# Expert tails as plain fp32 products in four column groups, and 160 rows per visit

## The reference

```
logits = h @ router_w + router_b                 # 1024 tokens, 32 experts
top_vals, top_idx = top_k(logits, 4); gates = softmax(top_vals)
for each expert e, on the tokens that chose it:
    gu  = x @ w_up[e] + b_up[e]                  # 1024 -> 2048
    glu = min(gu[:, :1024], 7); lin = clip(gu[:, 1024:], -7, 7)
    hid = glu * sigmoid(1.702 * glu) * (lin + 1)
    y   = hid @ w_down[e] + b_down[e]            # 1024 -> 1024
out[token] += gate * y
```

## Time and profile before

| what | value |
|---|---|
| time, median of 3 runs (lowest to highest) | 2607.01 us (2598.25 to 2608.39) |
| time of the profiled execution | 2605.41 us |
| its span, first to last instruction | 2603.6 us |
| mean granted TensorE clock | 0.954 |
| PE busy | 2385.3 us, 92% |
| DVE busy | 1812.7 us, 70% |
| ACT busy | 1293.2 us, 50% |
| HBM read and written | 484.37 MB and 41.68 MB |

### The profile page before, as it was taken

One profiled execution on the slowest core, in us unless ns is written; L12 is line 12 of the kernel. 1 busy time (PEld: TensorE's weight loads), 2 busy tenths in 40 slices (PEclk: granted clock), 3 DMA queues, 4 the chain that ended last, 5 costly groups with the idle time before them and its releaser, 6 DMA issues.

```text
span 2603.6 us, 38978 instructions
## 1 busy us (share of the span) xinstructions
PE 2385.3 (92%) x13604; PEld 1938.2 (74%) x13605; DVE 1812.7 (70%) x1928; ACT 1293.2 (50%) x1445; POOL 363.5 (14%) x305
## 2 busy tenths in 40 slices
PE   6999986699989977999999999999999999999993
PEld 4889864598748955777777777777777777777772
DVE  4699778514142465978877777778777778988763
ACT  5412364313231344766655555566555556766553
POOL 0000000010003011212112211221122112222111
PEclk8999987599999978999999999999999999999996
DMA  4111310310101148989978787689787789998775
GB/s 140 65 49 50 113 51 18 130 57 33 49 1 29 66 150 290 356 293 331 351 256 292 249 296 256 230 279 324 258 285 251 244 282 310 351 362 306 249 240 161
DMA packets 263968, 527.23 MB, mean 202 GB/s; under 512 B 10908, under 2 KB 45008, under 8 KB 263536
## 3 DMA queue, kind: packets, MB, share of 16 engines
q1 hardware_dynamic: 246976, 470.49, 51.3%
q0 software_dynamic: 15008, 52.70, 8.7%
q10 hardware_dynamic: 1904, 2.90, 0.4%
HBM read 484.37 MB, written 41.68 MB: 202 GB/s over the span
## 4 chain that ended last, share of the span: by engine, by line
PE 80%; DVE 8%; issue 6%; ACT 4%; DMA 1%; DVEq 1%; ACTq 0%; POOLq 0%; POOL 0%; SPq 0%
PE PS L2528 12%; PE PS L2530 12%; PE PS L2529 12%; PE PS L2094 9%; PE PS L2536 7%; PE PS L2533 6%; PE PS L2326 4%; PE PS L2424 4%; PE PS L2133 2%; DVE wlo L1886 2%; PE PS L2498 1%; PE PS L2386 1%; PE PS L2552 1%; PE PS L2351 1%; PE PS L2353 1%
## 5 line engine op out<-in xcount | busy, mean ns | idle before, releaser
L1886 DVE TENSOR_TENSOR wlo<-raw,whi 128x2048 fp32r<-128x2048 f32 x387 | 880.0, 2288 | 202.6 <-ACT whi L1128 182.1
L1128 ACT CAST whi<-raw 128x2048 fp32r<-128x2048 f32 x387 | 730.0, 1911 | 174.2 <-PE PS L2536 137.1
L2528 PE MATMUL PS<-whi,xhi 128*128 128x512 f32 x1024 | 426.4, 416 | 1.2 <-DVE wlo L1886 1.2
L2529 PE MATMUL PS<-wlo,xhi 128*128 128x512 f32 x1024 | 399.9, 391 | 1.8 <-issue 1.8
L2530 PE MATMUL PS<-whi,xlo 128*128 128x512 f32 x1024 | 401.4, 392 | 0.0
L2530 PEld LDWEIGHTS PS<-whi,xlo 128*128 128x128 f32 x1024 | 192.9, 188 | 44.4 <-issue 2.0
L2528 PEld LDWEIGHTS PS<-whi,xhi 128*128 128x128 f32 x1024 | 194.2, 190 | 40.8 <-DVE wlo L1886 7.5
L2529 PEld LDWEIGHTS PS<-wlo,xhi 128*128 128x128 f32 x1024 | 193.4, 189 | 38.7
L2528 PE MATMUL PS<-whi,hhi 128*128 128x512 f32 x512 | 203.5, 397 | 8.8 <-DVE wlo L1886 8.8
L2530 PE MATMUL PS<-whi,hlo 128*128 128x512 f32 x512 | 200.4, 391 | 0.0
L2529 PE MATMUL PS<-wlo,hhi 128*128 128x512 f32 x512 | 200.1, 391 | 0.0
(11 more groups left out here) (400 smaller groups left out, 4563.3 us busy)
## 6 DMA issues: line engine op xcount, KB each, us to landing
raw<-in_exp_w_up SPq DMA_DIRECT2D x259, 1024.0 KB, 5.1
raw<-in_exp_w_down SPq DMA_DIRECT2D x128, 1024.0 KB, 6.9
ring<-in_w_in SPq DMA_DIRECT2D x11, 1024.0 KB, 5.5
xres<-in_x SPq DMA_DIRECT2D x4, 1024.0 KB, 10.3
ring<-in_xattn_wk SPq DMA_DIRECT2D x4, 1024.0 KB, 9.1
ring<-in_xattn_wv SPq DMA_DIRECT2D x4, 1024.0 KB, 6.2
ring<-in_w_out SPq DMA_DIRECT2D x4, 1024.0 KB, 7.2
xres<-in_x SPq DMA_DIRECT2D x1, 4096.0 KB, 20.9
```

Source lines behind the costliest of these rows:

```text
L1128: nc.scalar.copy(whi[:, chunk_slot(c, NSPL), :], raw[chunk_slot(c, NRAW)][:]).then_inc(s_whi, 1)
L1886: nc.vector.tensor_tensor(wlo[:, chunk_slot(c, NSPL), :], raw[chunk_slot(c, NRAW)][:], whi[:, chunk_slot(c, NSPL), :].bitcast(F), ALU.subtract
L2528: pe.matmul(o, hi[:, k, :], wh, start=first and bias is None, stop=False)
L2529: pe.matmul(o, hi[:, k, :], wl, start=False, stop=False)
```

## The change

TAIL becomes 32 and CAP 160. A tail is no longer split into high and low parts: xtl and htl hold the turned 32 rows as plain fp32, and are multiplied with the loaded fp32 chunk in raw instead of whi and wlo. The 512 columns of a chunk are cut into four quarters of QC = 128; quarter j goes to output partitions 32j to 32j+31 of the tail's bank, so each quarter is a product of 32 columns of weights in another column group of the array. For each chunk all full-width products come first, then 16 products of 128 columns (4 k-tiles x 4 quarters), with four bias products of 128 columns at the group's start. tail_low, tail_sum, low_up, low_dn and their semaphores are gone; DVE reads each quarter from its 32 partitions into the right columns of partitions 0 to 31 (tail_quarters). row_gate's tail column is copied to all four partition groups. SP's load_chunk waits for PE to have multiplied the chunk six earlier, as PE now reads raw. The integer arithmetic that divides row numbers by 192 divides by 160.

```
-TAIL = P // 2
+TAIL = P // 4
+QC = 512 // 4
 CAP = P + TAIL
@@ load_chunk
-                    wait_lo(sp, t, c - NRAW)
+                    wait_multiplied(sp, t, c - NRAW)
@@ drain_rows (ACT)
-            def drain_rows(t, i, both, c0=9):
+            def drain_rows(t, i, c0=9):
                 cols = slice(512 * i, 512 * (i + 1))
...
+                wait_multiplied(act, t, c0 + 2 * i)
+                act.wait_ge(s_yst, 32 * t)
+                nc.scalar.copy(smx[:, 1, 2 + i:3 + i], smx[:, 0, 0:1])
+                nc.scalar.activation(yb[:, 0, cols], PS[:, 2 * i, :], ACT.Identity,
+                                     scale=row_gate[:, bass.ds(2 * t - 2, 1)]).then_inc(s_yev, 1)
@@ DVE
+            def tail_quarters(bank, dst, c0):
+                for j in range(4):
+                    yield dst[0:TAIL, 1, c0 + QC * j:c0 + QC * (j + 1)], PS[TAIL * j:TAIL * (j + 1), bank, 0:QC], j
@@ clamp_glu
-                    tail_sum(t, 2 * i, glu[0:TAIL, 1, :])
-                    dve.wait_ge(s_tsum, 4 * t + 2 * i + 1)
-                    ins = nc.vector.tensor_scalar(glu[0:TAIL, 1, :], glu[0:TAIL, 1, :], LIMIT, None, ALU.min)
+                    for to, part, j in tail_quarters(1, glu, 0):
+                        ins = nc.vector.tensor_scalar(to, part, LIMIT, None, ALU.min)
@@ tail_rows
+                    dve.wait_ge(s_yst, 32 * t)
                     for i in range(2):
-                        dve.wait_ge(s_low, 6 * t + low + i)
-                        nc.vector.scalar_tensor_tensor(out=yb[0:TAIL, 1, 512 * i:512 * (i + 1)],
...
+                        wait_multiplied(dve, t, c0 + 2 * i)
+                        for to, part, j in tail_quarters(2 * i + 1, yb, 512 * i):
+                            ins = nc.vector.tensor_scalar(to, part,
+                                                          row_gate[TAIL * j:TAIL * (j + 1), bass.ds(2 * t - 1, 1)],
+                                                          None, ALU.mult)
+                        ins.then_inc(s_yev, 1)
@@ products (PE)
-                    if tail:
-                        both_parts = tl[:, k].rearrange("p a c -> p (a c)")
-                        pe.matmul(ot, both_parts, wh, start=first, stop=False)
...
-                        ins = pe.matmul(ot, both_parts, wl, start=False, stop=stop and kk == 3)
+                if tail:
+                    quarters = [(PS[TAIL * j:TAIL * (j + 1), 2 * (i % 2) + 1, 0:QC], slice(QC * j, QC * (j + 1)))
+                                for j in range(4)]
+                    if begins and bias is not None:
+                        for ot, q in quarters:
+                            pe.matmul(ot, SEL[:, 0:TAIL], bias[:, q], start=True, stop=False)
+                    for kk in range(4):
+                        for ot, q in quarters:
+                            ins = pe.matmul(ot, tl[:, k0 + kk, :], raw[rslot][:, kk, q],
+                                            start=begins and kk == 0 and bias is None, stop=stop and kk == 3)
                 ins.then_inc(s_wmm, 1)
```

More of the change, by code:

```diff
@@ L1152, in hidden_hi @@
                     turned_hi(s_ht, t, hhi, htl, False, s_hhi)
[L1154 to L1170, removed]
             def expert_sigmoid(t, i, blocks):
@@ L1249, in _ @@
                 with act.If(t <= last_):
-                    both, both_last = has_tail(t), has_tail(t - 1)
+                    both = has_tail(t)
                     split_hi(t, 3)
@@ L1874, in _ @@
             pairs = lambda ap: ap.rearrange("p (v b) -> p v b", b=2)[:, :, 1]
-            step(nc.vector.tensor_copy(pairs(row_gate[TAIL:P, :]), pairs(PS[0:TAIL, 4, NB:2 * NB])))
+            for j in range(1, 4):
+                step(nc.vector.tensor_copy(pairs(row_gate[TAIL * j:TAIL * (j + 1), :]),
+                                           pairs(PS[0:TAIL, 4, NB:2 * NB])))
             def bias_selector(t):
@@ L1891, in has_tail, with turned_lo @@
                 return dve.value_load(VT[0:1, 1, bass.ds(t, 1)], min_val=0, max_val=1)
-            def turned_lo(t, split, hi, lo, tl, tail, done):
+            def turned_lo(t, split, hi, lo, done):
                 dve.wait_ge(split, t + 1)
@@ L1897, in turned_lo, with hidden_lo @@
                     ins = nc.vector.tensor_tensor(flat(lo, i), PS[:, 4 + i, :], flat(hi, i).bitcast(F), ALU.subtract)
-                if tail:
-                    ins = nc.vector.tensor_tensor(tl[:, :, 1, :], PS[:, 6, :].rearrange("p (k c) -> p k c", c=TAIL),
-                                                  tl[:, :, 0, :].bitcast(F), ALU.subtract)
                 ins.then_inc(done, 1)
             def tokens_lo(t):
[L1904 to L1921, removed]
+                turned_lo(t, s_xhi, xhi, xlo, s_xlo)
+            def hidden_lo(t):
+                turned_lo(t, s_hhi, hhi, hlo, s_hlo)
+            def tail_quarters(bank, dst, c0):
+                for j in range(4):
+                    yield dst[0:TAIL, 1, c0 + QC * j:c0 + QC * (j + 1)], PS[TAIL * j:TAIL * (j + 1), bank, 0:QC], j
             def nothing_to_add(done, count):
@@ L2036, in _ @@
                     tail_rows(t, both_last)
-                    hidden_lo(t, both)
+                    hidden_lo(t)
                     lo_by_vector(t + 1, 2)
@@ L2044, in _ @@
                             lo_by_vector(last_, c)
-                        tail_rows(last_ + 1, both_last, low=1)
+                        tail_rows(last_ + 1, both_last, c0=1)
             def final(t):
@@ L2519, in turn_hidden, with products @@
                     turn(hid, False, s_ht)
-            def products(i, tail, hi, lo, tl, k0, slot, begins, stop, bias=None):
-                o, ot = PS[:, 2 * (i % 2), :], PS[:, 2 * (i % 2) + 1, :]
+            def products(i, tail, hi, lo, tl, k0, slot, rslot, begins, stop, bias=None):
+                o = PS[:, 2 * (i % 2), :]
                 for kk in range(4):
@@ L2530, in products @@
                     ins = pe.matmul(o, lo[:, k, :], wh, start=False, stop=stop and kk == 3)
-                    if tail:
-                        both_parts = tl[:, k].rearrange("p a c -> p (a c)")
-                        pe.matmul(ot, both_parts, wh, start=first, stop=False)
-                        if first and bias is not None:
-                            pe.matmul(PS[0:TAIL, 2 * (i % 2) + 1, :], SEL[:, 0:TAIL], bias, start=False, stop=False)
-                        ins = pe.matmul(ot, both_parts, wl, start=False, stop=stop and kk == 3)
+                if tail:
[8 more added lines that the diff above has]
+                                            start=begins and kk == 0 and bias is None, stop=stop and kk == 3)
                 ins.then_inc(s_wmm, 1)
@@ L2555, in all_groups @@
                             wait_lo(pe, t, c)
-                            products(i, tail, xhi, xlo, xtl, 4 * half, chunk_slot(c, NSPL), half == 0, half == 1, bias)
+                            products(i, tail, xhi, xlo, xtl, 4 * half, chunk_slot(c, NSPL),
+                                     chunk_slot(c, NRAW), half == 0, half == 1, bias)
                 pe.wait_ge(s_xlo, t + 1)
@@ L2571, in all_groups @@
                             wait_lo(pe, t, c)
-                            products(i, tail, hhi, hlo, htl, 4 * half, chunk_slot(c, NSPL), half == 0, half == 1)
+                            products(i, tail, hhi, hlo, htl, 4 * half, chunk_slot(c, NSPL),
+                                     chunk_slot(c, NRAW), half == 0, half == 1)
                 pe.wait_ge(s_hlo, t)
```

66 lines of the change are left out of this document (16 added, 50 removed).

## The result

| | before | after |
|---|---|---|
| median of 4 runs on one chip (lowest to highest) | 2606.31 us (2598.25 to 2608.39) | 2986.22 us (2974.63 to 2992.02) |
| ratio, 95% interval | | 1.1459 [1.1411, 1.1506] |
| profiled execution; its span; mean granted clock | 2605.41; 2603.6; 0.954 | 2980.56; 2978.6; 0.883 |

The account below looks back on a forecast made before the run. PE was taken to bound the kernel, busy 92%, with DVE and transfers close in plain visits. 2605.4 + 75 - 146 - 12 + 10 = 2532 us; forecast 2505 to 2580 (65%), 8-in-10 range 2490 to 2620.

Parts of the forecast that it names:

- step 3: Tail products on PE: four column groups stream side by side, a tail falls from 25.6 to 15.9 us; -146 us.
- step 6: Weight loads: chunks are held until PE has multiplied them, so loads start later; +10 us, bounds 0 and 68.
- Step 1: Visits: 160 rows make 34 instead of 32, each extra one costing a plain visit; +75 us.
- Step 2: Tail's present cost on PE: 25.6 us summed, against 23.1 to 24.5 measured by difference.
- Step 4: Bank hand-over from DVE to PE: waits for yb shrink as DVE reads four quarters after the last product; -12 us.
- Step 5: DVE and ACT beside the tail: DVE loses 7.2 us and gains 7.2 per tail; 0 us.
- Fewer column groups: Rival on narrow tail products: two of four groups side by side, 2692 us; 12% together with one after the other.
- weight loads in the path: Rival on narrow tail products: their weight loads add 0.8 us a chunk, 144 us in all; 2676 us, 4%.
- passes one after the other: Rival case on narrow tail products: no column groups overlap, 2986 us; within the 12% for fewer groups side by side.
- The clock did fall: Rival: PE's clock falls as narrow products leave it less busy, doubling plain visits' PE work; over 3000 us, 2%.
- Plain visits over 39 us: Sign that the forecast is wrong; plain stretches between first bias products were expected at 37 to 38.5 us.

Follow-up runs that it names:

- e1: The changed kernel with PE's last down part moved out of the loop's else branch to behind the loop; 2565.93 us, ratio 0.9855.
- e4: e1 with the tail branch taken per chunk, full-width products written once and narrow ones first; 2541.74 us, ratio 0.974.
- e8: e4 with SP's loads waiting on a semaphore raised by PE's first full-width product of a chunk, not the last; 2527.75 us, ratio 0.9699.
- e7: The kernel before with CAP = 160, its 64-row tail and products unchanged; 2683.86 us, ratio 1.0294.
- e3: The kernel before with SP's weight loads waiting until PE has multiplied the chunk six earlier; 2617.92 us, ratio 1.0044.
- e11: e9 with 62 never-run products ahead of the loop, moving it by 126 instructions; 3235.09 us, ratio 1.2423.
- e9: The kernel before with two never-run copies of the last down part inside the loop's executed path; 2615.59 us, ratio 1.0042.
- e10: The kernel before with one never-run copy of the last down part inside the loop's executed path; 2603.23 us, ratio 0.9996.
- e2: The kernel before with three never-run copies of the last down part at the loop's end; 2624.23 us, ratio 1.0063.

## Why the prediction was wrong

**The step that failed** is in step 3: "handing them out costs 32 x 0.0086 = 0.28 us a chunk, no bound". It counted the time to hand the passes out and not their code. 32 passes with their loads are 64 instructions a chunk, and they took the loop from 4.8 blocks to 7.8. No rival had it. The one term that is missing is +420 us (after against e1), and without it the sum stands: where 2532 was forecast, e1 takes 2565.93 us, e4 2541.74 and e8 2527.75 (e8 has its chunks given back earlier, so the 10 us of step 6 are not in it). The profile before had the row that could have raised the question, 59 instruction loads that end with the first visits, and I made nothing of it.

**The other steps**, measured one by one:
- Step 1, two more visits: +75 forecast, +78 measured (e7).
- Step 2, what a tail cost: right by the difference below.
- Step 3, the price of the new tail. In e8 the full-width products of one chunk's end and the next one's start, with the narrow ones between:

```profile
1908.58 0.39 PE L2482 MATMUL PS<-wlo,xhi 128*128 128x512 f32 x1
1908.80 0.39 PE L2483 MATMUL PS<-whi,xlo 128*128 128x512 f32 x1
1909.12 1.08 PE L2494 MATMUL PS<-raw,xtl 128*32 128x128 f32 x32
1910.13 0.50 PE L2479 MATMUL PS<-whi,xhi 128*128 128x512 f32 x1
1910.47 0.40 PE L2482 MATMUL PS<-wlo,xhi 128*128 128x512 f32 x1
```

  From 1908.80 to 1910.47 are 1.67 us for two starts that otherwise take 0.46: 1.21, the forecast's 0.90 + 0.31. Single records show four passes starting within 0.02 us and the next four 0.11 us after them (the second round 0.13). Between turnings of hidden rows, a stretch with both tails falls from 60.5 us on average to 51.2 in e8, one with an up tail from 54.2 to 46.6, with a down tail from 45.1 to 41.9: 6 x 9.3 + 9 x 7.6 + 9 x 3.3 = 154 us, where steps 3 and 4 had 158 together (the 15th tail's down part, the last of all, lies outside these stretches and is counted at the same price). The plain ones stay: 37.3 and 37.4 us in the median. Only the first of them, in which the last blocks are still being loaded, is shorter, 38.3 for 42.8 us; with it the 8 lose 6 us, which no step had.
- Step 4, the hand-over: PE's waits for yb fell from 16.4 us to 10.3 in e8 (6.1 and 4.2), so 6 us and not 12 (it is within the 154). DVE's quarters take 0.28 us where they are clamped and 0.34 where they are scaled, against 0.30 taken and the 0.28 of the earlier trace rows; of e8 (mean ns behind the busy time):

```profile
L1920 DVE TENSOR_SCALAR yb<-PS,row_gate 32x128 f32<-32x128 f32 x120 | 41.3, 344 | 23.7 <-PE PS L2483 22.4
L1902 DVE TENSOR_SCALAR hid<-PS 32x128 f32<-32x128 f32 x120 | 33.8, 282 | 1.2
```

- Step 5, DVE and ACT beside it: nothing shows against 0; DVE is busy 42.6 of 47.2 us in the up-tail stretch of e4, and no wait of PE for it is larger than before.
- Step 6, the longer hold: +10 forecast, +10.1 measured (e3), and e8 takes at least that back, 14 us under e4.

Put together: 2605.9 (before, on the chip of e8) + 78 - 154 - 6 = 2524; e8 has 2527.75.

**The rivals.** Fewer column groups and weight loads in the path are refuted by 1.05 us for 32 passes: four groups run side by side, and their loads vanish. That the result lies on the 2986 us that the prediction gave to passes one after the other is chance; those would show 3.4 us a chunk. The Trainium skill, "TensorE: Matmul & The Clock Gate", states that weight loads run beside products in flight only where the row group differs, and measures 2.38 times for three column tiles, 79% each. The first this trace does not bear out: here all four groups have the same rows, and the 32 loads of a chunk, 0.11 us each, cost nothing beside the products. The second it does with latency counted: 3.42 us of passes take 1.05, 3.3 of four or 81% each; in steady rounds (0.107 of a pass alone against 0.109 for four) it is 3.9 of four. The clock did fall, in after, but behind the gaps, not because of the narrow products: in e4 and e8 it is 1.00 in stretches with both tails. "Plain visits over 39 us" was named as what would prove the forecast wrong, and it did: 49.8 on average in after.

**What stays open.** That PE stands still until a block has landed is read from the order in time of loads and restarts; no semaphore ties a gap to its load. Why seven blocks stay and not eight, why e11's loads cost 2.3 us and not 1.7, and where exactly the edges of the blocks lie, was not tried. e1 is 24 us slower than e4 at 70 loads against 62. In the profiled executions, 14 us apart, the stretches of the first three visits alone are 21 us longer in e1, and they hold its additional loads; so most of it is code that is loaded for the first time. In stretches with both tails the two take the same 51.2 us, so e4's 12 conditions a visit cost nothing that shows there.

## What to carry to other kernels

Count instructions as well as their time: an fp32 product is four, and in a loop with its bodies written out for each branch they multiply. Read the row of the instruction queue, before and after: if its loads go on through the loop, the code that a turn passes over doesn't stay, and the cure is to move what runs once out of the loop and to branch around the part that differs, not around copies of the whole. When a large loss comes with "issue" as its releaser, test it with code that never runs, placed inside and outside the executed path.

## What the runs showed of the hardware

- A PE loop whose turns touch up to seven blocks of 16 KB of instructions is not fetched again (59 to 62 loads in before, e4, e9 and e10, 70 in e1 and e2); with eight it is, in most visits (197 to 368 loads), for 1.7 to 2.3 us a load. The counts of seven and eight hold with the offset inferred at e11. The Trainium skill's 128 KiB ("Runtime: NRT & Kernel Launch", "Instruction fetch mechanics") would be eight blocks; the runs found room for seven.
- Moving a loop by 126 instructions, with code that never runs, changed the time from 2615.59 to 3235.09 us.
- Such a gap costs twice: 10.85 us of standing still, and then products at half the rate: six starts from 2001.78 to 2004.57 take 2.79 us instead of 1.38.
- Four fp32 tiles of 128 rows by 32 columns stream side by side at nearly full rate: a round of four passes of 128 columns every 0.109 us, where one pass alone takes 0.107.
